# A diffusion backbone on one core: two weight tiles prepared ahead, VectorE's work in another order, and one weight load moved to another DMA queue

## The reference, cut to what matters

```python
def swiglu(h, wg, wu, wd):
    return (jax.nn.silu(h @ wg) * (h @ wu)) @ wd

# per layer i:
xs = layer_norm(ALPHA * xs + g1 * yx, ln_g[i, 0], ln_b[i, 0])
xs = layer_norm(ALPHA * xs + g2 * swiglu(xs * (1.0 + sc2) + sh2, ffn_wg[i], ffn_wu[i], ffn_wd[i]), ...)
# layer 0 only: the same for the context stream cs
# layer 1, the "latents" of the attention, from modulated hx and hc:
cq  = rms_norm(hx @ mla_wdq, gq)
ckv = rms_norm(h @ mla_wdkv, gkv)       # both streams
kr  = h @ mla_wkr                       # both streams, then rotary
```

## Time and profile before

| | |
|---|---|
| time, median of 3 runs | 3408.88 us (3405.33 to 3414.22) |
| profiled execution: time, span | 3408.59 us, 3406.9 us |
| mean granted TensorE clock | 0.972 |
| TensorE busy | 3183.0 us (93%) |
| VectorE, ScalarE, GpSimd busy | 2163.4 (64%), 1290.3 (38%), 313.0 us (9%) |
| DMA | 413.78 MB, mean 121 GB/s |

### The profile page before, as it was taken

The page is one execution under the profiler, slowest core; times in us unless marked ns, Lnnn a source line. Parts: engine busy times, 40 slices in busy tenths (PEclk is TensorE's granted clock), DMA queues, the critical chain, the costliest instruction groups (busy, mean ns, idle before and its releaser), DMA issues.

```text
span 3406.9 us, 49323 instructions
## 1 busy us (share of the span) xinstructions
PE 3183.0 (93%) x19122; PEld 2488.8 (73%) x19122; DVE 2163.4 (64%) x3218; ACT 1290.3 (38%) x2124; POOL 313.0 (9%) x508
## 2 busy tenths in 40 slices
PE   7999979998898999999999889999999899999897
PEld 3888645555676888888787757777778578888785
DVE  6989855555467555455767656666566666566766
ACT  3221333333335323333445444444343353333344
POOL 0111245544100000000000200000000000000000
PEclk8999999999898999999999999999999999999999
DMA  7655656678512223225434410000012143334532
GB/s 293 207 201 200 220 164 186 188 193 222 176 63 86 81 81 99 78 81 202 150 98 158 146 59 17 21 12 17 12 31 81 50 142 96 105 108 166 178 102 87
DMA packets 186046, 413.78 MB, mean 121 GB/s; under 512 B 33695, under 2 KB 60639, under 8 KB 183143
## 3 DMA queue, kind: packets, MB, share of 16 engines
q1 hardware_dynamic: 133640, 274.23, 24.7%
q0 software_dynamic: 51936, 131.27, 12.8%
q10 hardware_dynamic: 288, 5.77, 0.4%
HBM read 262.90 MB, written 81.00 MB: 101 GB/s over the span
## 4 chain that ended last, share of the span: by engine, by line
PE 76%; DVE 12%; DMA 4%; ACT 3%; issue 3%; POOL 1%; SPq 1%; DVEq 0%; ACTq 0%; POOLq 0%
PE ps L660 19%; PE ps L661 19%; PE ps L662 19%; PE ps L2510 2%; PE ps L2528 2%; PE ps L2619 2%; PE ps L2384 2%; PE ps L730 2%; PE ps L2584 1%; PE ps L2549 1%; PE ps L2580 1%; DMA traw<-hidden_scratch 1%; DMA t2k<-s 1%; PE ps L2593 1%; DVE mx L2995 1%
## 5 line engine op out<-in xcount | busy, mean ns | idle before, releaser
L660 PE MATMUL ps<-HB,gsp 128*128 128x512 f32 x1232 | 488.1, 396 | 37.1 <-DVE HB L836 21.9
L661 PE MATMUL ps<-HB,gsp 128*128 128x512 f32 x1232 | 484.6, 393 | 0.0
L662 PE MATMUL ps<-HB,gsp 128*128 128x512 f32 x1232 | 483.2, 392 | 0.0
L1121 DVE TENSOR_TENSOR gsp<-graw,gsp 128x512 fp32r<-128x512 f32 x330 | 226.4, 690 | 262.4 <-ACT gsp L1100 261.6
L1100 ACT ACTIVATE gsp<-graw 128x512 fp32r<-128x512 f32 x330 | 206.6, 628 | 326.4 <-PE ps L662 266.6
L660 PEld LDWEIGHTS ps<-HB,gsp 128*128 128x128 f32 x1232 | 234.1, 190 | 90.3 <-issue 21.4
L662 PEld LDWEIGHTS ps<-HB,gsp 128*128 128x128 f32 x1232 | 233.9, 190 | 49.8
L661 PEld LDWEIGHTS ps<-HB,gsp 128*128 128x128 f32 x1232 | 234.3, 190 | 46.5 <-issue 1.0
L660 PE MATMUL ps<-tsp,wdh 128*128 128x512 f32 x616 | 242.9, 394 | 18.3 <-DVE tsp L1382 18.3
L662 PE MATMUL ps<-tsp,wdh 128*128 128x512 f32 x616 | 241.5, 392 | 0.0
L661 PE MATMUL ps<-tsp,wdh 128*128 128x512 f32 x616 | 241.4, 392 | 0.0
(11 more groups left out here) (288 smaller groups left out, 7265.3 us busy)
## 6 DMA issues: line engine op xcount, KB each, us to landing
graw<-in_w_gu SPq DMA_DIRECT2D x176, 256.0 KB, 2.7
mring<-in_mod_w POOLq DMA_DIRECT2D x78, 512.0 KB, 4.7
hidden_scratch<-R SPq DMA_DIRECT2D x154, 256.0 KB, 2.4
traw<-hidden_scratch SPq DMA_DIRECT2D x154, 256.0 KB, 2.7
t2k<-s POOLq DMA_DIRECT2D x80, 256.0 KB, 5.9
t2z<-s POOLq DMA_DIRECT2D x160, 128.0 KB, 3.8
t2w<-w POOLq DMA_DIRECT2D x160, 128.0 KB, 3.3
wraw<-in_w_in SPq DMA_DIRECT2D x48, 256.0 KB, 4.4
```

The costliest lines, as they stand in the source:

```text
L660: pe.matmul(o, wh, xh, start=start, stop=False, skip_group_check=onto)
L661: pe.matmul(o, wh, xl, start=False, stop=False, skip_group_check=onto)
L662: return pe.matmul(o, wl, xh, start=False, stop=stop, skip_group_check=onto)
L1121: dve.tensor_tensor(gsp[U % 3][:, 1, :], graw[:, q, W_SLOT[i], :], gsp[U % 3][:, 0, :].bitcast(F32), ALU.subtract).then_inc(w.lo, 1)
```

## The change

Four edits. (1) **Latents.** Latent tiles 0 and 1 get raw buffers of their own (`lat_raw`), tile 0 also its own split buffers (`lat_hi`, `lat_lo`); both are loaded while the context product still runs, tile 0 is split before its end, tile 1 in the middle of the additions behind it; tiles 2 and on go the old way. (2) **The first three low parts of gate-up** are made before the last addition of the output projection, not behind it. (3) **Order at the start of gate-up**: the first weight sums stand before `inverse`, not between it and `normed`; each low part of block 2 follows its token sums at once; the two groups of four `residual` instructions of ScalarE move from units (2,0) and (2,1) to (2,1) and (3,0). (4) **`wd[1]`** is issued by ScalarE, on its queue, before its splits of step v = 2, and not by SP. (2) to (4) hold for both layers.

```diff
+        lat_raw = [place(f"lat_raw{i}", k, [P, KD, P]) for i, k in enumerate((132, 136))]
+        lat_hi, lat_lo = place("lat_hi", 140, [P, KD, P], F32R), place("lat_lo", 144, [P, KD, P], F32R)
...
-                if j >= 2:
-                    block_low(dve, w, 2, j - 2)
-            block_low(dve, w, 2, 2)
-            block_low(dve, w, 2, 3)
+                block_low(dve, w, 2, j)
...
             for t in range(KD, mix_tiles(l)):
+                if t == mix_tiles(l) - 1:
+                    for U in range(3):
+                        gu_split_lo(dve, wn[l], U)
                 mix_out(dve, l, t, count)
...
-            gu_split_lo(dve, wn[l], 0)
...
-                if not more:
-                    down_third(sp, w)
...
-                if n == 0 and i == 2:
-                    for k in range(4 * q, 4 * q + 4):
+                if n == 0 and (i, q) in ((2, 1), (3, 0)):
+                    for k in range(4 * (i - 2), 4 * (i - 2) + 4):
                         residual(act, L1, k, R[:, k, L1.cols])
...
-            gu_split_lo(dve, w, 1)
-            gu_split_lo(dve, w, 2)
             centre(dve, L1, 2)
...
                 if n == 0 and (i, q) == (0, 0):
-                    inverse(dve, L1)
                     for q_ in range(2):
                         gu_sums(dve, w, 0, q_, True)
+                    inverse(dve, L1)
                     normed(dve, L1)
...
+            if v == 2:
+                act.wait_ge(w.done, w.DONE + w.unit(NP - 1, 5, 1) + 1)
+                act.wait_ge(w.lo, w.W + w.units)
+                act.dma_start(wd[1][:], a["w_dx"][w.l, 1]).then_inc(w.raw[0][2], 16)
...
+            lat_low(dve, 0)
             for m in range(KD):
+                if m == 4:
+                    lat_low(dve, 1)
...
+        def lat_high(act, t):
+            for h in range(2):
+                act.wait_ge(p_mla.raw[h], 16 * (p_mla.loads + t + 1))
+                if t == 0:
+                    act.wait_ge(s_cd, NF - 2)
+                else:
+                    act.wait_ge(s_cdone, KD)
+                act.activation(lat_hi[:, 4 * h:4 * h + 4, :] if t == 0 else whi[h][:], lat_raw[t][:, 4 * h:4 * h + 4, :], ACT.Copy
+                               ).then_inc(p_mla.hi, 1)
+
+        def lat_low(dve, t):
+            for h in range(2):
+                hi, lo = (lat_hi[:, 4 * h:4 * h + 4, :], lat_lo[:, 4 * h:4 * h + 4, :]) if t == 0 else (whi[h][:], wlo[h][:])
+                dve.wait_ge(p_mla.hi, p_mla.base + 2 * t + h + 1)
+                dve.tensor_tensor(lo, lat_raw[t][:, 4 * h:4 * h + 4, :], hi.bitcast(F32), ALU.subtract).then_inc(p_mla.lo, 1)
...
         def latents_sync(sp):
+            for t in range(2):
+                sp.wait_ge(Stream.lo, CTX_W + NF - 4 + t)
+                for h in range(2):
+                    if t:
+                        sp.wait_ge(p_mla.hi, p_mla.base + h + 1)
+                    sp.dma_start(lat_raw[t][:, 4 * h:4 * h + 4, :], wtile(a["w_lat"], LATENT_TILES[t][1])[:, 4 * h:4 * h + 4, :]
+                                 ).then_inc(p_mla.raw[h], 16)
             sp.wait_ge(s_cdone, KD)
             for t, (c, m) in enumerate(LATENT_TILES):
-                tile_load(sp, p_mla, t, wtile(a["w_lat"], m))
+                if t == 2:
+                    for h in range(2):
+                        sp.wait_ge(p_mla.hi, p_mla.base + 2 + h + 1)
+                        sp.dma_start(wraw[h][:], wtile(a["w_lat"], m)[:, 4 * h:4 * h + 4, :]).then_inc(p_mla.raw[h], 16)
+                elif t > 2:
+                    tile_load(sp, p_mla, t, wtile(a["w_lat"], m))
...
         def latents_act(act):
             Lc = norms[1, 2]
-            act.wait_ge(s_cdone, KD)
-            tile_high(act, p_mla, 0)
+            lat_high(act, 0)
+            lat_high(act, 1)
...
         def latents_dve(dve):
             Lc = norms[1, 2]
-            dve.wait_ge(s_cdone, KD)
-            tile_low(dve, p_mla, 0, 0)
-            tile_low(dve, p_mla, 0, 1)
```

More of the change, by code:

```diff
@@ L708, in tile_low, with tile_pe @@
             dve.tensor_tensor(wlo[h][:], wraw[h][:], whi[h][:].bitcast(F32), ALU.subtract).then_inc(sm.lo, 1)
-        def tile_pe(pe, sm, t, n, x, ready):
+        def tile_pe(pe, sm, t, n, x, ready, parts):
             for h in range(2):
@@ L717, in tile_pe @@
                     hi, lo = x(k)
-                    mm = mm3(pe, bank(t % 2, n), whi[h][:, k % 4, :], wlo[h][:, k % 4, :], hi, lo, k == 0, k == KD - 1)
+                    wh, wl = parts(t, h)
+                    mm = mm3(pe, bank(t % 2, n), wh[:, k % 4, :], wl[:, k % 4, :], hi, lo, k == 0, k == KD - 1)
                 mm.then_inc(sm.full, 1)
@@ L1323, in down_second @@
             sp.dma_start(wd[2][:], a["w_dx"][w.l, 2]).then_inc(w.raw[0][3], 16)
-        def down_third(sp, w):
-            sp.wait_ge(w.done, w.DONE + w.unit(NP - 1, 5, 1) + 1)
-            sp.wait_ge(w.lo, w.W + w.units)
-            sp.dma_start(wd[1][:], a["w_dx"][w.l, 1]).then_inc(w.raw[0][2], 16)
         def down_sync(sp, w):
@@ L1577, in build, with lat_parts @@
         RMS_BANK, KROPE_BANK = (2, 3, 6, 7, 2), (5, 0, 1)
+        def lat_high(act, t):
[12 more added lines that the diff above has]
+                dve.tensor_tensor(lo, lat_raw[t][:, 4 * h:4 * h + 4, :], hi.bitcast(F32), ALU.subtract).then_inc(p_mla.lo, 1)
+        def lat_parts(t, h):
+            if t == 0:
+                return lat_hi[:, 4 * h:4 * h + 4, :], lat_lo[:, 4 * h:4 * h + 4, :]
+            return whi[h], wlo[h]
         def latent_place(t):
@@ L1652, in ready @@
                         pe.wait_ge(L.h, L.H + k + 1)
-                tile_pe(pe, p_mla, t, L.n_, lambda k: (HsM[:, k, 0, L.cols], HsM[:, k, 1, L.cols]), ready)
+                tile_pe(pe, p_mla, t, L.n_, lambda k: (HsM[:, k, 0, L.cols], HsM[:, k, 1, L.cols]), ready, lat_parts)
                 if t == 1:
@@ L1669, in latents_act @@
             Lc = norms[1, 2]
-            act.wait_ge(s_cdone, KD)
-            tile_high(act, p_mla, 0)
+            lat_high(act, 0)
+            lat_high(act, 1)
             for t in range(W_LAT):
-                if t + 1 < W_LAT:
+                if 1 <= t < W_LAT - 1:
                     tile_high(act, p_mla, t + 1)
```

## The result

The changed kernel takes 3394.66 us (median of 6 runs, 3389.88 to 3399.62) against 3413.52 for the kernel before (6 runs of its own in the same series, 3405.33 to 3416.11). The ratio is 0.9947, 95% interval 0.9937 to 0.9956. Run once more beside the first experiments it came to 0.9955 (0.9942 to 0.9968). The prediction, 3384.9 against 3408.6, is a ratio of 0.9930: faster, as forecast, but a gain of 18 us (0.0053 x 3410; 15.0 to 21.5 by the interval) instead of 23.7. In absolute time it is 9.8 us above the forecast and 0.7 us above its range; 4.9 of the 9.8 are the kernel before itself, which took 3413.52 us in this series and not the 3408.6 that the forecast started from. The profiled execution took 3394.8 us (span 3393.1).

The account below looks back on a forecast made before the run. TensorE, busy 93% of the span, was taken as the bound, so only its waits and low clock could pay. Gains of 11.5 + 6.2 + 5.5 + 0.5 = 23.7 us off 3408.6 gave 3384.9, range 3373 to 3394.

Parts of the forecast that it names:

- Edit 1: Latents: TensorE's 8.8 us wait goes and the clock stays full, 2.75 more; taken as 11.5 us, between 8.8 and 11.8.
- edits 2 and 3: Start of gate-up: low parts first and the new order gain 3.1 us per layer (2.5 to 5.1), 6.2 in two.
- 2.17 + 2.5 - 0.3 = 4.4: Gate-up, per layer: 2.17 us from low parts first, 2.5 from earlier weight sums, 0.3 lost on block 2's low parts.
- The new wait: Gate-up: TensorE gets early to unit (5,0), waits 3.5 us before it, and the clock falls there.
- The move's cost: Gate-up: moving the residual groups loses 1.3 us per layer in the sum (1.4 in the working), or gains 0.7 if the clock holds.
- edit 4 in layer 0: Down product, layer 0: v = 4's wait goes and v = 7 starts 6.6 us earlier; gain 5.5 us, bounds 3 and 10.6.
- v = 4 lands about 1606 and its wait is gone: Down product, layer 0: the load of v = 4, issued before `wd[1]`, lands about 1606, so TensorE no longer waits for it.
- the rule of turns: DMA queues take turns packet by packet, so a 2 KB row costs its queue one turn against a 22 KB row.
- edit 4 in layer 1: Down product, layer 1: v = 4 still lands with the large packets' end, about 3165.5; gain 0.5 us, bounds -1 and 12.2.
- The down edit buys nothing: Rival, down product: ScalarE's second large issue is held while its queue is full; 3391 to 3398 us, chance 13%.
- The wait goes in both layers: Rival, down product: hidden loads get through between large packets, 10.6 and 12.2 us; 3368 in all; whole or large part 17%.
- stay low through the start of gate-up: Slower rival: new short waits keep the clock low from unit (2,0) on, 2.4 us per unit; 3419 with 14 more, chance 2%.

Follow-up runs that it names:

- the first experiments: The kernel before with only the latents edit, only the two gate-up edits, or only the `wd[1]` edit: ratios to before 0.9966, 0.9977 and 1.0006.
- e1_latents: The kernel before with the latents edit alone: 3400.95 us, ratio to before 0.9966.
- e3_down: The kernel before with only `wd[1]` moved to ScalarE's queue: 3413.81 us, ratio to before 1.0006.
- e9_blocks_late: The changed kernel, rows still 22 KB, with ScalarE issuing `wd[1]` at step v = 4 and `wd[3]` at v = 5: 3381.66 us, ratio to before 0.9920.
- e14_block_at_v3: The changed kernel with `wd[1]` issued by ScalarE at step v = 3, directly ahead of `wd[3]`, rows of 22 KB: 3391.28 us, ratio to before 0.9938.
- e15_block_behind_v4: The changed kernel with ScalarE waiting at step v = 2 for v = 4's load to land before issuing `wd[1]`: 3391.21 us, ratio to before 0.9937.
- e12_rows_2k_late: The changed kernel with `wd[1]` and `wd[3]` loaded in rows of 2 KB and `wd[3]` issued at step v = 5: 3375.74 us, ratio to before 0.9886.

## Why the prediction was right or wrong

**Right in kind: faster, by the latents above all.** Edit 1 was put at 11.5 us (8.8 to 11.8). Alone it measures 11.6 (7.5 to 15.7), by the table 10.5 to 11.8. Every link held: no wait, clock 1.00, tile 2 hidden. Matmul against matmul, every kernel with edit 1 has won 11.6 us at 1926 and still at 1965; then TensorE waits 3.5 us for squares, before as after, and the six matmuls behind that wait took 5.49 us in the changed kernel (granted clock 0.50) and 4.33 before (0.64). That is where 11.6 became the table's 10.5.

**Right: edits 2 and 3.** Put at 3.1 us per layer. By the table, in kernels with the changed order, 2.0 to 3.3 in layer 0 (1.3 more if held against `e1_latents` and `e3_down`, whose unedited stage was slower than that of before) and 1.6 to 4.5 in layer 1; alone 7.8 for 6.2 in sum. Behind unit (2,1), before the residual groups act, all of these kernels have won 3.8 us in layer 0 and 4.3 in layer 1, for 2.17 + 2.5 - 0.3 = 4.4 forecast. The new wait was forecast at 3.5 us before (5,0) and is 3.21 and 3.22, and the clock falls behind it. The move's cost, forecast at 1.3, is 1.3 to 1.5 in layer 0 in most traces and 0.2 in two. (The prediction's own working gives 1.4 for the move, where its sum takes 1.3, with a unit at the low clock at 2.1 us, where it elsewhere has 2.4; 12 matmuls at 0.2 are 2.4.)

**Wrong: edit 4 in layer 0, put at 5.5 us, measured nothing (-0.4 to 1.3 by the table in the kernels that have the edit and the old rows, 0.0 to 0.3 in those without the edit; -2 and 3.4 either way for both layers by `e3_down`).** This step carries the missing gain: 23.7 less 5.5 is 18.2, and 18 was measured. The failed step is "v = 4 lands about 1606 and its wait is gone": v = 4 landed at 1622.4 in the times of before, and the wait was 8.09 us. The prediction had just said that by the rule of turns moving `wd[1]` "doesn't free the loads behind it"; it then counted on an order of issue instead. Three things in that fell:

- *The order.* "Both before `wd[1]` starts: ScalarE issues it at 1603.8." Moved by the 2.9 us between the two executions, SP issued the context's store at 1602.8, just as forecast, but ScalarE issued `wd[1]` at 1602.3, not 1603.8, ahead of both.
- *What "before" has to mean.* With v = 4 issued 0.4 us behind the store, as it was, the forecast had it some 0.6 us ahead of `wd[1]`, and took that for served first. Ahead of the blocks a load lands 2.5 to 4.1 us after its issue (`e9_blocks_late`, `e14_block_at_v3`, `e15_block_behind_v4`); `e15_block_behind_v4`, with a lead of 3.7 us, frees v = 4. Whether a lead between 0 and 3.7 us would do wasn't tried.
- *The arithmetic behind the order.* With the order given, v = 7 started at 1626.7 in `e15_block_behind_v4`, 1629.9 in the times of before, against 1628.0 forecast and 1634.6 before: 4.7 us earlier instead of 6.6. The 13 matmuls at the low clock behind that wait cost 2.6 us (0.2 each) and the first behind it 0.3, where the forecast took off 1.1. That leaves the table's 1.7. So in this trace this order is worth 1.7 us, not 5.5; it isn't quite the forecast's, since `wd[1]` went out at 1606.9 in the times of before, 3 us later than assumed. What the turns give to v = 4 they take from v = 7, unless the blocks go out later still, as in `e9_blocks_late` (7.1 us).

**Nearly right: edit 4 in layer 1, put at 0.5.** In the traces with edit 4 and the old rows the stage gains 0.2 to 2.0 us, without it 0.5 to 1.9. Nothing can be told from nothing there, and v = 4 waits 8.7 us still, as forecast for it (8 to 10). The prediction's words for layer 1, that v = 4 "lands with their end", hold for both layers: v = 4 landed 0.3 us behind `wd[3]` in layer 0 and 0.5 in layer 1. A v = 4 behind the large ones in layer 0 too is what this step should have forecast.

**The rivals.** "The down edit buys nothing" had 13%, with 3391 to 3398, and is what happened; its mechanism, ScalarE held in its second issue, is not (0.33 us), though it is real with rows of 2 KB. "The wait goes in both layers" was sized rightly, at 22.8 us, and needs small rows and a later `wd[3]`. Small rows with `wd[1]` left on SP's queue and `wd[3]` late, or `wd[3]` alone moved, weren't tried. The clock did not stay low through the start of gate-up.

## What to carry to other kernels

Moving a large transfer to another queue need not free those behind it, if its packets are larger than theirs: here a row of 22 KB cost each load of the other queue about ten times its own turn, and cutting the rows to 2 KB, with no byte less, was worth 9.9 us in layer 0 where the move alone was worth nothing. Issuing it later, when the small ones have landed, is the other cure: with the large rows it was worth 7.1 us there. A wait with a fall of the clock behind it costs more than its length (in layer 0, 3.7 us of waits were 6.9 us of time), so a helper's work goes into its engine's idle time first, before it is weighed against another wait. And when two profiles are compared, unedited stages differ between executions, here by up to 6 us in the first 1000 and by 2 in stretches of 250, so gains are read stage by stage and confirmed by single edits.

## What the runs showed of the hardware that was not expected

- An engine can be held in the issue of a DMA while earlier ones are outstanding in its queue: two transfers with rows of 2 KB, 2.9 MB together, took ScalarE 3.81 and 7.69 us to issue (layers 0 and 1) when they came 5 us behind another such pair, and 2.58 and 1.61 when they came 11 us behind it. The one transfer with rows of 22 KB took 0.33. That it is the number of outstanding rows, and not the state of the engines, is argued from these and wasn't tried by itself.
- The low clock behind the same wait lasts unequally. Behind the wait of 3.2 us before (5,0) in layer 1, five matmuls ran at the low level in the changed kernel's profile, and all 12 of the window below in that of `e12_rows_2k_late`, whose instructions are the same there. It is 1.4 of the 2.8 us between 4.4 and 1.6 in the table (7 more at 0.2 us); the rest was lost ahead of 2680, in stages that no edit touches. Behind the wait of 2.3 us before (4,0) the clock stayed at 1.00 in 17 of 20 places (ten kernels with the changed order, two layers) and fell within the unit behind in 3. The window of `e12_rows_2k_late`:

```profile
2731.50:2737.00 5.50, 5.26 (x12) 4.18 (x13) 5.47 (x10) 3.23 (x6) 0.90 (x1) 0.50 0.74 181
```
